# Matmuls without a use in nine idle stretches of TensorE, in a fused two-block transformer kernel

## What is computed

```python
# first kind, two layers (mod = silu(c) @ w_mod + b_mod gives shift, scale, gate)
h = rms_norm(x, norm1) * (1.0 + scale1) + shift1
proj = h @ w_in                      # pool inputs, q, three k/v pairs, gates
y_pool = pool_mixer(u, pool_w, pool_scale)
y_nsa = nsa_mixer(q, k_all, v_all, gates, ...)  # compressed, selected, window branches
x = x + gate1 * (concat([y_pool, y_nsa]) @ w_out)
h2 = rms_norm(x, norm2) * (1.0 + scale2) + shift2
x = x + gate2 * (square(relu(h2 @ w_ff1)) @ w_ff2)
# second kind, one layer
u = h @ w_in_2                       # z, xbc, dt, q, k, v, gate logits
mix = (gates0 * (ssd_branch(...) @ w_proj_ssd) + gates1 * (attention_branch(q, k, v) @ w_proj_attn)) @ w_out
h = layer_norm(alpha * h + mix)
h = layer_norm(alpha * h + square(relu(h @ w_up)) @ w_down)
```

## Time and profile before

| | us |
|---|---|
| median of 3 runs | 1336.99 |
| range of the runs | 1334.86 to 1337.26 |
| span of the profiled execution | 1329.4 |
| TensorE matmul busy | 1241.3 (93%) |
| VectorE busy | 933.6 (70%) |
| ScalarE busy | 620.7 (47%) |

### The profile page before, as it was taken

The page is one execution under the profiler, slowest core; times in us unless marked ns, Lnnn a source line. Parts: engine busy times, 40 slices in busy tenths (PEclk is TensorE's granted clock), DMA queues, the critical chain, the costliest instruction groups (busy, mean ns, idle before and its releaser), DMA issues.

```text
span 1329.4 us, 21440 instructions
## 1 busy us (share of the span) xinstructions
PE 1241.3 (93%) x8834; PEld 1140.5 (86%) x8834; DVE 933.6 (70%) x1223; ACT 620.7 (47%) x828; POOL 48.2 (4%) x54
## 2 busy tenths in 40 slices
PE   6699999999999999999999998998889997999997
PEld 6688879998988888999998987886779986899996
DVE  5888787768879885855557469878865554755553
ACT  2444344444443624444444443488875523544432
POOL 1004000000000320000000000000000000000000
PEclk8799999999989999999999998999989988999999
DMA  9752366667666315455555532446644442455520
GB/s 379 300 228 96 130 250 242 234 255 282 246 242 246 135 64 201 159 187 179 181 219 207 190 127 95 158 162 228 224 177 148 175 159 95 159 191 189 181 105 32
DMA packets 43631, 247.84 MB, mean 186 GB/s; under 512 B 4160, under 2 KB 12368, under 8 KB 15520
## 3 DMA queue, kind: packets, MB, share of 16 engines
q1 hardware_dynamic: 43104, 244.57, 49.8%
q0 software_dynamic: 448, 2.14, 0.4%
HBM read 245.58 MB, written 1.11 MB: 186 GB/s over the span
## 4 chain that ended last, share of the span: by engine, by line
PE 70%; DVE 16%; DMA 7%; ACT 4%; issue 3%; SPq 0%; POOL 0%; DVEq 0%; ACTq 0%
PE bank L419 14%; PE bank L421 14%; PE bank L420 14%; PE bank L722 11%; PE bank L723 5%; DMA arena<-in_modw 5%; DVE ring_w L414 4%; PE bank L805 2%; DVE macc L1057 2%; DVE arena L1958 1%; PE bank L846 1%; DVE arena L1057 1%; ACT w_hi L409 1%; DMA arena<-dscr 1%; PE bank L514 1%
## 5 line engine op out<-in xcount | busy, mean ns | idle before, releaser
L414 DVE TENSOR_TENSOR ring_w<-raw,w_hi 128x2048 fp32r<-128x2048 f32 x170 | 389.4, 2294 | 159.3 <-ACT w_hi L409 158.6
L409 ACT ACTIVATE w_hi<-raw 128x2048 fp32r<-128x2048 f32 x170 | 323.9, 1909 | 139.7 <-PE bank L421 123.0
L722 PE MATMUL bank<-act,w_hi 128*128 128x512 f32 x768 | 281.8, 408 | 17.1 <-DVE arena L1340 5.9
L419 PE MATMUL bank<-act,w_hi 128*128 128x256 f32 x800 | 236.4, 295 | 8.8 <-DVE act L1078 7.2
L419 PE MATMUL bank<-ff_hi,w_hi 128*128 128x256 f32 (+1 forms) x816 | 230.9, 283 | 1.0 <-issue 1.0
L421 PE MATMUL bank<-ff_hi,ring_w 128*128 128x256 f32 (+1 forms) x816 | 231.3, 283 | 0.0
L420 PE MATMUL bank<-ff_lo,w_hi 128*128 128x256 f32 (+1 forms) x816 | 231.3, 283 | 0.0
L420 PE MATMUL bank<-act,w_hi 128*128 128x256 f32 x800 | 228.8, 286 | 0.0
L421 PE MATMUL bank<-act,ring_w 128*128 128x256 f32 x800 | 228.5, 286 | 0.0
L723 PE MATMUL bank<-act,ring_w 128*128 128x256 f32 x768 | 218.1, 284 | 0.0
L722 PEld LDWEIGHTS bank<-act,w_hi 128*128 128x128 f32 x768 | 146.5, 191 | 57.1 <-issue 10.9
(11 more groups left out here) (324 smaller groups left out, 1695.2 us busy)
## 6 DMA issues: line engine op xcount, KB each, us to landing
raw<-in_panels SPq DMA_DIRECT2D x170, 1024.0 KB, 4.8
arena<-in_modw SPq DMA_DIRECT2D x48, 1024.0 KB, 6.8
mixf<-dscr SPq DMA_DIRECT2D x8, 512.0 KB, 4.3
arena<-dscr SPq DMA_DIRECT2D x8, 512.0 KB, 4.9
mixf<-dscr SPq DMA_DIRECT2D x8, 256.0 KB, 5.7
arena<-dscr SPq DMA_DIRECT2D x8, 256.0 KB, 6.1
cst<-in_cst SPq DMA_DIRECT2D x1, 1251.5 KB, 7.8
arena<-in_x SPq DMA_DIRECT2D x1, 1024.0 KB, 5.1
```

The lines of the kernel that those rows point to most:

```text
L409: nc.scalar.activation(w_hi[slot(k)][:, :], w_raw(m, k), ACT.Copy).then_inc(hi_done, 1)
L414: nc.vector.tensor_tensor(w_lo(m, k), w_raw(m, k), w_hi[slot(k)][:, :].bitcast(F32), ALU.subtract).then_inc(lo_done, 1)
L419: nc.tensor.matmul(o, wh, xh, start=start, stop=False, skip_group_check=skip)
L722: nc.tensor.matmul(bank[4 + c][:, :], wh[:, s:s + P], act2[:, kc, :, :], start=kc == 0, stop=False)
```

## The change

A helper `pe_fill(pe, o, n)` issues n matmuls of a bf16 identity with itself, four times side by side (512 columns), into bank `o`. Nobody reads the result. It is called in six places of the source; two of them run in both layers and one at two attention units, so that there are nine bursts in an execution and 81 matmuls. In the attention slots the wait for `s2_p` is moved behind the waits for the copies and behind the fill.

```diff
--- before.py
+++ after.py
@@ -487,6 +487,13 @@
                     last.then_inc(rows_done, 1)
             return last
 
+        def pe_fill(pe, o, n):
+
+
+            eyes = idb[:, :].unsqueeze(1).to_broadcast([P, 4, P])
+            for _ in range(n):
+                nc.tensor.matmul(o[:, :], idb[:, :], eyes, start=True, stop=True, skip_group_check=True)
+
         def pe_out(pe, m, k, steps=(0, 16)):
 
             pe.wait_ge(lo_done, 4 * m + k + 1)
@@ -573,6 +580,7 @@
                 pe_used(pe, pe_panel(pe, m, k, G(g), act_hi, act_lo, arrive if g == 0 else None))
 
             pe_gfree(pe, l, 2)
+            pe_fill(pe, G(2), 7)
             pe.wait_ge(lo_done, 4 * m + L_V1V2 + 1)
             wh, wl = w_hi[slot(L_V1V2)], w_lo(m, L_V1V2)
             for tt in range(TT):
@@ -701,10 +709,12 @@
             pe_norm_sum(pe, 2 * l + 1, (0, 1, 2, 3))
             mod(5)
             pe_norm_sum(pe, 2 * l + 1, (4, 5, 6, 7))
+            pe_fill(pe, bank[0], 9)
             pe.wait_ge(modc_ready, 3 * l + 3)
             pe_ff(pe, l, m, lambda kc: pe.wait_ge(act_ready, 16 * l + KC + kc + 1), 16 * l, L_FF, "ahead" if ahead else "tail")
             if ahead:
                 pe_norm_sum(pe, 2 * l + 2)
+                pe_fill(pe, bank[0], 9)
 
         def pe_ff(pe, l, m, arrive, j0, k0, mods=None):
 
@@ -1544,7 +1554,6 @@
                     last.then_inc(dt_tr, 1)
                 if i in ATT_SLOT:
                     u = ATT_SLOT[i]
-                    pe.wait_ge(s2_p, u + 1)
                     if u:
 
                         pe.wait_ge(s2_ev0, u)
@@ -1552,6 +1561,9 @@
                     if u == 4:
                         pe.wait_ge(s2_lo, 1)
                         pe.wait_ge(dt_cols, 1)
+                    if u in (3, 7):
+                        pe_fill(pe, bank[6], (12, 6)[u // 4])
+                    pe.wait_ge(s2_p, u + 1)
                     for n in range(6):
                         last = nc.tensor.transpose(bank[6 + n // 4][:, (n % 4) * P:(n % 4 + 1) * P], pp[u % 2][:, n * P:(n + 1) * P], ident)
                     last.then_inc(s2_tr, 1)
@@ -1638,6 +1650,7 @@
                 pe_used(pe, pe_panel_rows(pe, M2, 38 + n, bank[0:4], lambda kk: hi[:, c + kk, :], lambda kk: lo[:, c + kk, :], n == 0, n == 7,
                                           parts=n == 7))
             pe.wait_ge(att_proj, 4)
+            pe_fill(pe, bank[4], 7)
             for n in range(4):
                 if n == 2:
                     pe.wait_ge(x2_ready, 2)
@@ -1646,6 +1659,7 @@
                 pe_used(pe, pe_panel(pe, M2, 46 + n, bank[4 + n % 2], mix_hi, mix_lo,
                                      (lambda kc: pe.wait_ge(mx_lo, kc // 2 + 1)) if n == 0 else None))
             pe_layer_norm(pe, 0)
+            pe_fill(pe, bank[0], 15)
             pe_ff(pe, layers, M2, lambda kc: pe.wait_ge(ln_lo, kc + 1), 16 * layers, 50)
             pe_layer_norm(pe, 1)
             for c in range(4):
```

## The result

The changed kernel takes 1338.95 us (median of 20 runs, 1334.96 to 1352.09); the kernel before, run beside it, 1335.84 us (median of 20, 1330.69 to 1337.91). The ratio is 1.0038, with a 95% interval from 1.002 to 1.0055: 5.1 us slower, 2.7 to 7.3. The two medians alone are 3.1 apart and the two means 4.7, because a few runs of the changed kernel are long (three of 20 above 1347). The predicted 1341.6 is 2.7 above the measured median, which lies in the range of 1337.0 to 1345.0, and the sign was right.

A forecast was written before the change was run, and what follows sets the result against it. TensorE, busy 93% of a 1329.4 us span, was taken as the bound. Late terms of 5.9 less 1.3 back gave +4.6, 1334.0; with the median's 7.6 above the span, 1341.6 us, range 1337.0 to 1345.0.

The forecast's parts named there:

- A fill behind the wait costs its whole length (V1V2): Before the V1V2 panels: fills start only after the wait, 1.7 us late in layer 0, 1.6 in layer 1.
- The slots (+2.6): Attention units 3 and 7: fills start after the copy wait, making real work 1.2 and 1.4 us late.
- the rival of the swallowed part: Behind the attention slots: later waits for VectorE absorb the slots' 2.6 us, giving 1339.0; chance 0.15.
- The feed-forward parts and the layer change (0 to 0.4): Fills hide in these gaps; VectorE paces what follows, so 0 to 0.4 us back each, nothing for layer 0's feed-forward.
- The output projection (0 to 1.7, taken 0.9): Before the output projection: fills fit the gap; dense half-clock work behind speeds up, at most 1.7 us back, half taken.
- the case that the step named: Output projection: nothing gained if the thin stretch before 1086.15 lets the clock fall again.
- The sum: Whole kernel: 5.9 us late minus 1.3 back, net +4.6 on the profiled span.
- The rival of the held clock: V1V2 and slot fills run in idle time and the clock stays full: 7.2 us back, 1329.8; chance 0.07.
- The fill's price: Every burst: 0.23 us per 512-column fill at full clock, 0.44 at half; the skill's 131 ns would forecast 1339.3.

The follow-up runs named there:

- slots: Only the bursts of attention units 3 and 7, behind their waits, added to the kernel before: 1336.72 us, ratio 0.9999.
- fixed9: All nine bursts, the V1V2 and slot ones moved ahead of the waits that make their gaps, against the kernel before: 1335.76 us, ratio 0.9994.
- best6: Five early bursts plus V1V2 bursts moved ahead of their wait, none in the attention slots, against the kernel before: 1333.12 us, ratio 0.9973.
- v1v2_7: Only the two V1V2 bursts of seven fills, behind their wait, added to the kernel before: 1337.83 us, ratio 1.0034.
- late4: Only the four bursts behind their waits (V1V2, units 3 and 7), against the kernel before: 1341.63 us, ratio 1.0043; timed again 1338.23 us, 1.003.
- v1v2_x2: Only the two V1V2 bursts, behind their wait, with 14 fills each instead of 7, against the kernel before: 1341.86 us, ratio 1.0038.
- early5: Only the five bursts ahead of their waits (feed-forward parts, layer change, output projection), against the kernel before: 1333.26 us, ratio 0.9977.
- best7: Five early and moved V1V2 bursts, plus three fills at two waits inside the output projection's first panel, against the kernel before: 1333.77 us, 0.9992.

## Why the prediction was right, point by point

- *A fill behind the wait costs its whole length (V1V2).* Right by the stages, and the loss is with these bursts. Predicted +3.3 for both; the stages show +1.45 in each layer, 2.9 in all, and twice that for twice the fills. In the timed runs the fourteen cost what the stages say; the seven cost nothing in seven runs of 12 and some 11 us in five, which no length of a burst explains. The step also took the split that ends at 57.1 for this panel's; by the order of VectorE's program that is the next panel's, and this one's had ended at 54.9, which changes nothing. Layer 0 was taken at half clock (7 × 0.44, then 1.4 won back), layer 1 at 0.23 a fill; what the rows show is 7 × 0.21 in both, whether the clock is low there or not. A burst at the lower clock takes longer (2.61 us) and pushes work out of the low stretch, as the step said, and the two come out at the same 1.45.
- *What that term lacked.* The low stretch behind the gap comes and goes by itself, at 1.5 us. The prediction had it in layer 0 and not in layer 1, as the one profile of before had it; two profiles of the same program have it in different layers. In the changed kernel's profile it stands in both, which makes +2.95 in layer 1 out of 1.45. A burst behind the gap doesn't keep it away; it was there at six of ten such gaps with the burst behind the wait, at six of 12 with no burst, and at none of six with the burst ahead (the table above). So it adds nothing to the late bursts' price on average.
- *The slots (+2.6).* The mechanism was right (the bursts start when L1989 has ended, the gaps are still 3.71 and 1.83 us), and the term was too big: 0.1 on average and 1.25 by the stages, and by the timed runs of `slots` alone at most 1.5 in all. At unit 3 the step priced 1.2 against the one profile of before, whose low stretch there was 6.8 us; against that one the burst costs 0.6 to 0.9, and against the five kernels with 10.2 us it costs nothing or saves up to 0.6. TensorE reaches the transposes behind L1948 12.1 to 12.4 us behind the gap with the burst and 11.5 to 12.7 without, and never under 11.5, where VectorE's chain ends. That chain is a floor, in the manner of the rival of the swallowed part, at a place that it didn't name: it had the waits for the mixf tiles in mind. Unit 7 has no such cover; its 1.25 doesn't show in the timed runs, which is within their interval.
- *The feed-forward parts and the layer change (0 to 0.4).* Right. The steps behind the gap stay 0.79 apart at the full clock, as in the earlier trace rows at half. These rows are of the changed kernel:

```profile
537.71 0.50 PE L732 MATMUL bank<-act,w_hi 128*128 128x512 f32 x1
...
538.50 0.50 PE L732 MATMUL bank<-act,w_hi 128*128 128x512 f32 x1 [0.18 <-DVE act L1088]
...
539.29 0.50 PE L732 MATMUL bank<-act,w_hi 128*128 128x512 f32 x1 [0.18 <-DVE act L1088]
```

  With the 15 fills of the last part these bursts give 0.9994, nothing that can be told. From the layer norm's sums to the last part's first matmul it is 13.02 us with its burst and without, and from there to the end 206.7 to 206.8.
- *The output projection (0 to 1.7, taken 0.9).* Right in kind: 1.3 us on average by the stages, up to 2.2 between two single profiles where 1.7 was the most, 0.15% of the time by itself. In the changed kernel's own profile it is 0.2, since the clock fell again in the first panel, the case that the step named.
- *The sum.* Predicted +4.6; measured 5.1 (2.7 to 7.3). The terms as measured are V1V2 +2.9, slots 0 to +1.5, early bursts −3.1 (0.9977): −0.2 to +1.3. The long runs add 1.6 to the changed kernel's mean, which makes 1.4 to 2.9, at the lower end of what the whole measures. The total was closer than its parts, and part of the agreement is luck: the slots cost about half of the 2.6 that was taken, the early bursts gave back 3.1 where 1.3 was taken (their stages show 1.3, and the floor is 2), and what makes up for both are in part the long runs that came with the late ones, of which the prediction has nothing, and in part a remainder that no run explains. The 7.6 us between the profiled execution and the median, too, were put down to launch and end; a run's time is 2.1 us above its own span, and the rest is that the profiled execution was a fast one.
- *The rival of the held clock.* Wrong for the changed kernel, whose rows show the waits in front of the fills. The kernels with the bursts moved show that it is the right idea in the wrong place, and smaller than it looks: 7.2 us was its worth by the half-clock time, 3.6 us is the best that was measured. Of the difference, unit 3's 3.2 us lie behind VectorE (`fixed9`). The Trainium skill's advice to leave no long idle gaps between bursts of matmuls, so that throughput doesn't drop (TensorE: Matmul & The Clock Gate, section "Why this matters for your kernels"), agrees with `best6` (clock 0.976, ratio 0.9973). In the changed kernel four gaps of 1.8 to 3.7 us are as idle as before, and the fills behind them cost time: the clock is 0.971 and the ratio 1.0038.
- *The fill's price.* 0.23 was taken; the bursts show 0.19 to 0.215 at the upper clock. The Trainium skill's page on TensorE, section "Back-to-back issue gap", has about 131 ns for 512 columns in a stream; the rows here don't agree (14 fills in 2.84 us, 0.20 each). By the Trainium skill's figure the V1V2 terms would have been under 2, an estimate. By the measured one they fall from 3.3 to 2.9.

**What stays open.** Timed runs of the kernels that have the V1V2 bursts of seven behind the wait fall into two groups. Long are five of 12 of `v1v2_7` at 1344.1 to 1348.7 with a mean clock of 0.954 to 0.958 (the other seven are at 1334.5 to 1339.0 with 0.963 to 0.967); two of 12 and three of 12 of the two runs of `late4`; three of 20 of the changed kernel. `slots`, `v1v2_x2`, `early5`, `best6` and the kernel before have no such group; `best7` has one run of 1344.7, with 0.966. The clock is enough to explain the size (0.0085 of 1345 us is 11.4 us of full clock, the groups are some 11 apart), but no profile caught such an execution, so where in it the clock is low isn't known, nor why fourteen fills don't bring it about. It is 1.6 to 4.6 us of the mean of these kernels. Open with it is why the seven short runs of `v1v2_7` don't show the 2.9 us of its stages.

## What to carry to other kernels

A fill can be free only where it stands in the program ahead of the wait that makes the gap, and even there it isn't sure to pay: the nine bursts of `fixed9` all stand so (0.9994), and the seven of `best6` bring more (0.9973). Look up the releaser of the gap in the timeline, find its semaphore, and put the fill before that wait, into a bank that this wait doesn't guard. Price the held clock by what paces the work behind the gap: where another engine fed TensorE tile by tile here, or its chain ended the next wait, half the clock cost next to nothing and holding it returned next to nothing. Judge such a change by time; here the mean granted clock rose while the kernel became slower.

## What the hardware showed that was not expected

- The low stretches are not all fixed to the program. The same kernel before had the clock at 0.50 behind the V1V2 gap of layer 0 in one profile and of layer 1 in the next, 1.5 us each time; a single pair of profiles can differ by that at a gap of this kind, with nothing changed. Behind the gaps ahead of the feed-forward parts and between the layers it was low in 24 of 24 cases without a burst ahead of the wait, and in one of 18 with it.
- A matmul of 512 bf16 columns takes 0.19 to 0.215 us in a burst at the upper clock, nearly what one with float32r operands takes (0.23).
- Two gaps of the same 2.44 us at the same place of the program, each with the same seven fills behind it, had different clocks behind them: 0.50 in the changed kernel (64.53), 1.00 in `v1v2_7` (63.53, the fills in 1.33 us). The length of the gap alone didn't say what the clock does.
